# Pairwise sums of squares before the sums on TensorE, a later wait for the inverse root in two FFN blocks, and rows spread by two rounded products

## The reference, cut to what matters

```python
def rmsnorm(x, g):
    xf = x.astype(F32)
    y = xf * lax.rsqrt(jnp.mean(xf * xf, axis=-1, keepdims=True) + RMS_EPS)
    return (y * g.astype(F32)).astype(x.dtype)

def swiglu(h, w_in, w_out):
    a, b = jnp.split(h @ w_in, 2, axis=-1)
    return (jax.nn.silu(a) * b) @ w_out
...
        x = x + g1 * rmsnorm(y_lat, norm_g[l, 1])
        f_lat = swiglu(rmsnorm(x, norm_g[l, 2]) * (1.0 + sc2) + sh2, ffn_w_in[l], ffn_w_out[l])
...
    # gated_delta_rule, layer 3: g and beta are one row of 256 tokens for each of the 8 heads
    gc = jnp.cumsum(g, axis=-1)
    diff = gc[..., :, None] - gc[..., None, :]
    decay = jnp.where(tril, jnp.exp(jnp.where(tril, diff, 0.0)), 0.0)
    kb = k * beta[..., None]
    lmat = jnp.where(strict, jnp.einsum('nbhid,nbhjd->nbhij', kb, k) * decay, 0.0)
```

## Time and profile before

| | us |
|---|---|
| median of 3 runs | 2207.27 |
| lowest and highest | 2203.91, 2208.76 |
| the profiled execution | 2202.34 |
| its span in the trace | 2200.5 |
| TensorE busy | 2129.5 (97%) |
| VectorE busy | 1416.4 (64%) |
| ScalarE busy | 996.8 (45%) |
| GpSimd busy | 178.0 (8%) |

### The profile page before, as it was taken

The page is one execution under the profiler, slowest core; times in us unless marked ns, Lnnn a source line. Parts: engine busy times, 40 slices in busy tenths (PEclk is TensorE's granted clock), DMA queues, the critical chain, the costliest instruction groups (busy, mean ns, idle before and its releaser), DMA issues.

```text
span 2200.5 us, 32199 instructions
## 1 busy us (share of the span) xinstructions
PE 2129.5 (97%) x13450; PEld 1831.8 (83%) x13450; DVE 1416.4 (64%) x1612; ACT 996.8 (45%) x1124; POOL 178.0 (8%) x94
## 2 busy tenths in 40 slices
PE   6999998999999999999999999999999999989999
PEld 4887787888888856888888898888988897878888
DVE  4267974766756456666666678666666688566665
ACT  3322353544544244444544555445544566254444
POOL 0065600000000000000100011000100012001000
PEclk8999999999999999999999999999999999999999
DMA  8227924455455412455555534555455543124552
GB/s 337 97 96 301 421 88 146 170 189 190 163 190 188 157 72 77 155 189 191 196 189 190 189 134 144 191 191 191 156 190 190 190 154 116 41 87 172 191 191 77
DMA packets 52609, 373.28 MB, mean 170 GB/s; under 512 B 5792, under 2 KB 6816, under 8 KB 7968
## 3 DMA queue, kind: packets, MB, share of 16 engines
q1 hardware_dynamic: 51632, 367.71, 45.8%
q0 software_dynamic: 880, 4.19, 0.6%
HBM read 370.84 MB, written 1.05 MB: 169 GB/s over the span
## 4 chain that ended last, share of the span: by engine, by line
PE 45%; DVE 3%; ACT 2%; POOL 0%; issue 0%; ACTq 0%; DVEq 0%
PE PS L376 13%; PE PS L380 7%; PE PS L395 4%; PE PS L396 4%; PE PS L397 4%; PE PS L299 3%; PE PS L1498 1%; PE PS L286 1%; PE PS L288 1%; PE PS L287 1%; PE PS L2184 1%; DVE ring_r L500 1%; PE PS L1667 0%; PE PS L1769 0%; POOL X L1464 0%; PE PS L1457 0%
## 5 line engine op out<-in xcount | busy, mean ns | idle before, releaser
L500 DVE TENSOR_TENSOR ring_r<-ring,AR_r 128x2048 fp32r<-128x2048 f32 x290 | 664.5, 2298 | 263.8 <-ACT AR_r L494 263.6
L494 ACT ACTIVATE AR_r<-ring 128x2048 fp32r<-128x2048 f32 x290 | 552.6, 1911 | 327.2 <-PE PS L397 196.0
L376 PE MATMUL PS<-AR_r 128*128 128x512 f32 x2240 | 533.2, 390 | 0.0
L376 PEld LDWEIGHTS PS<-AR_r 128*128 128x128 f32 x2240 | 415.6, 188 | 83.1
L380 PEld LDWEIGHTS PS<-AR_r,ring_r 128*128 128x128 f32 x2240 | 287.2, 191 | 10.9
L380 PE MATMUL PS<-AR_r,ring_r 128*128 128x256 f32 x2240 | 290.6, 283 | 0.0
L541 ACT ACTIVATE AR<-PS 128x512 f32<-128x512 f32 x140 | 83.7, 598 | 420.5 <-PE PS L380 420.5
L396 PE MATMUL PS<-ring_r,AR_r 128*128 128x512 f32 x616 | 241.2, 392 | 0.0
L395 PE MATMUL PS<-AR_r 128*128 128x512 f32 x616 | 241.2, 392 | 0.0
L397 PE MATMUL PS<-AR_r 128*128 128x512 f32 x616 | 240.3, 390 | 0.0
L603 DVE TENSOR_TENSOR AR<-AR,PS 128x512 f32<-128x512 f32 x70 | 48.1, 687 | 141.3 <-ACT AR L541 141.3
(11 more groups left out here) (412 smaller groups left out, 2941.3 us busy)
## 6 DMA issues: line engine op xcount, KB each, us to landing
ring<-stream SPq DMA_DIRECT2D x346, 1024.0 KB, 4.8
X<-xt SPq DMA_DIRECT2D x1, 2048.0 KB, 9.7
AR<-bias POOLq DMA_DIRECT2D x1, 1536.0 KB, 7.0
AR<-pt POOLq DMA_DIRECT2D x2, 512.0 KB, 4.7
out<-X SPq DMA_DIRECT2D x4, 256.0 KB, 2.1
AR<-invc SPq DMA_DIRECT2D x1, 512.0 KB, 15.3
X<-negl POOLq DMA_DIRECT2D x1, 512.0 KB, 7.4
H<-wax POOLq DMA_DIRECT2D x1, 512.0 KB, 7.7
```

Of the source, the lines that this page charges most:

```text
L376: pe.matmul(PS[:, (6, 4)[half] + j, :], block(w_hi_of(tag, i + half), j, k), X_PARTS[:, k, :], start=(k == 0), stop=False, skip_group_chec ...
L494: act.activation(w_hi_of(tag, i), ring[:, n % SLOTS, :], ACT.Identity).then_inc(split_hi, 1)
L500: dve.tensor_tensor(RING_R[:, n % SLOTS, :], ring[:, n % SLOTS, :], w_hi_of(tag, i), ALU.subtract).then_inc(split_lo, 1)
```

## The change

1. **Pairs.** For the five later sums VectorE first adds the squares of the two feature tiles of a pair (new function `dve_pair_squares`, four TENSOR_TENSOR of 128x256, after `dve_add_turned`), and `pe_norm` makes four products in place of eight. The two sums that open the kernel stay.
2. **A sum one chunk earlier.** ("ffn0_pre", 0) now stands between the context chunks 1 and 2 of mixer 0's output projection, not between 2 and 3.
3. **A later wait in the two FFN blocks.** `sums` no longer waits for `rinv`. Banks 1 to 3 are opened at once, `down(0, 4, ...)` begins with them, and only ahead of bank 0 come the wait for `rinv` and the opening of bank 0.
4. **Rounded spreads.** ScalarE rounds ROWS to ROWS_HI once (8x512), VectorE makes ROWS_LO (8x512) and a rounded copy of the identity's corner (8x8), during the projections of mixer 3; `spread(h)` is two fp32r products of 512 columns in place of one in full fp32.

```diff
+            else:
+                for q in range(GROUPS):
+                    pe.wait_ge(S["paired_squares"], S.at("paired_squares", (tag, q)))
+                    ins = pe.matmul(PS[:, bank, 0:T], ONES, SQ[:, 2 * q, cols], start=(q == 0), stop=(q == GROUPS - 1))
             ins.then_inc(S["feature_sums"], S.mark("feature_sums", tag))
+        def dve_pair_squares(dve, tag, cols):
+            for q in range(GROUPS):
+                dve.wait_ge(S["squares"], S.at("squares", (tag, q)))
+                dve.tensor_tensor(SQ[:, 2 * q, cols], SQ[:, 2 * q, cols], SQ[:, 2 * q + 1, cols], ALU.add).then_inc(
+                    S["paired_squares"], S.mark("paired_squares", (tag, q)))
...
+                for t, h in ((0, 1), (1, 0), (1, 1), (0, 0)) if open_first else ((0, 0), (0, 1), (1, 0), (1, 1)):
+                    if open_first and (t, h) == (0, 0):
+                        open_first()
...
-                sums()
-                open_sums()
+                summed = sums()
+                for b in range(1, 4):
+                    pe.matmul(PS[:, b, 0:2], ZERO[:, :], ZERO[:, 0:2], start=True, stop=False, skip_group_check=True)
+                def open_first():
+                    pe.wait_ge(S["rinv"], S.at("rinv", summed))
+                    pe.matmul(PS[:, 0, 0:2], ZERO[:, :], ZERO[:, 0:2], start=True, stop=False, skip_group_check=True)
                 pe.wait_ge(ffn_gated, g0 + 1)
-                down(0, 4, False, 0)
+                down(0, 4, False, 0, open_first)
...
             out_chunk(1, ctx)
+            pe_norm(pe, ("ffn0_pre", 0), LAT, 0)
             out_chunk(2, ctx)
-            pe_norm(pe, ("ffn0_pre", 0), LAT, 0)
             out_chunk(3, ctx)
...
-                pe.matmul(PS[:, SPREAD_BANKS[h % 4], :], bc(IDENT[0:DH, h:h + 1], [DH, P]), ROWS[0:DH, :, :], start=True, stop=True).then_inc(S["row_spread"], S.mark("row_spread", h))
+                pe.wait_ge(S["cols_taken"], S.at("cols_taken", "rows split"))
+                row = bc(ONE_OF[0:DH, h:h + 1], [DH, P])
+                pe.matmul(PS[:, SPREAD_BANKS[h % 4], :], row, ROWS_HI[0:DH, :, :], start=True, stop=False)
+                pe.matmul(PS[:, SPREAD_BANKS[h % 4], :], row, ROWS_LO[0:DH, :, :], start=False, stop=True).then_inc(S["row_spread"], S.mark("row_spread", h))
...
+                    act.wait_ge(S["beta3"], S.at("beta3"))
+                    act.activation(ROWS_HI[0:DH], ROWS[0:DH], ACT.Identity).then_inc(S["rows3"], S.mark("rows3", "rounded"))
...
+                    dve.wait_ge(S["rows3"], S.at("rows3", "rounded"))
+                    dve.tensor_tensor(ROWS_LO[0:DH], ROWS[0:DH], ROWS_HI[0:DH], ALU.subtract).then_inc(order.sem, order.step())
+                    dve.tensor_copy(ONE_OF[0:DH], IDENT[0:DH, 0:DH]).then_inc(S["cols_taken"], S.mark("cols_taken", "rows split"))
...
             dve_add_turned(dve, order, "mix1_post", HIGH, LAYER1 + G_MIXOUT, 0)
+            dve_pair_squares(dve, "ffn1_pre", LAT)
             dve_modulate(dve, order, "ffn1_pre", 0, LAYER1 + G_FFN, LAYER1 + SH_FFN, "ffn1_lat")
```

More of the change, by code:

```diff
@@ L227, in pe_norm @@
             bank = norm_bank(cols) if bank is None else bank
-            for k in range(DT):
-                if k % 2 == 0:
-                    pe.wait_ge(S["squares"], S.at("squares", (tag, k // 2)))
-                ins = pe.matmul(PS[:, bank, 0:T], ONES, SQ[:, k, cols], start=(k == 0), stop=(k == DT - 1))
-            ins.then_inc(S["feature_sums"], S.mark("feature_sums", tag))
+            if tag[0] == "mix0":
+                for k in range(DT):
+                    if k % 2 == 0:
+                        pe.wait_ge(S["squares"], S.at("squares", (tag, k // 2)))
+                    ins = pe.matmul(PS[:, bank, 0:T], ONES, SQ[:, k, cols], start=(k == 0), stop=(k == DT - 1))
+            else:
+                for q in range(GROUPS):
+                    pe.wait_ge(S["paired_squares"], S.at("paired_squares", (tag, q)))
+                    ins = pe.matmul(PS[:, bank, 0:T], ONES, SQ[:, 2 * q, cols], start=(q == 0), stop=(q == GROUPS - 1))
+            ins.then_inc(S["feature_sums"], S.mark("feature_sums", tag))
+        def dve_pair_squares(dve, tag, cols):
[3 more added lines that the diff above has]
+                    S["paired_squares"], S.mark("paired_squares", (tag, q)))
         ADA_GROUPS, ADA_FIRST = 24, 4
@@ L2033, in build @@
         COLS = arena(24064, 2, 3, DH)
+        ROWS_HI, ROWS_LO = arena(24192, 2, T, of=AR_R), arena(23040, 2, T, of=AR_R)
+        ONE_OF = arena(24704, DH, of=AR_R)
         NA = TMP[0:DH, 0:2]
@@ L2642, in sums @@
                 pe_norm(pe, tag, cols, 0)
-                pe.wait_ge(S["rinv"], S.at("rinv", tag))
+                return tag
             for t in range(1):
@@ L2812, in _ @@
             dve_add_turned(dve, order, ("mix0_post", 0), LOW, G_MIXOUT, 0)
+            dve_pair_squares(dve, ("ffn0_pre", 0), LAT)
             dve_modulate(dve, order, ("ffn0_pre", 0), 0, G_FFN, SH_FFN, "ffn0_lat")
@@ L2815, in _, with add_and_pair @@
             dve_split_chunk(dve, "ffn0_lat", 2)
-            dve_ffn(dve, "ffn0_lat", lambda: dve_add_turned(dve, order, ("mix0_post", 1), LOW, G_MIXOUT, 1),
+            def add_and_pair(tag, g, s, nxt):
+                dve_add_turned(dve, order, tag, LOW, g, s)
+                dve_pair_squares(dve, nxt, STREAM[s])
+            dve_ffn(dve, "ffn0_lat", lambda: add_and_pair(("mix0_post", 1), G_MIXOUT, 1, ("ffn0_pre", 1)),
                     lambda: dve_modulate(dve, order, ("ffn0_pre", 1), 1, G_FFN, SH_FFN))
@@ L2822, in _ @@
             dve_split_chunk(dve, "ffn0_ctx", 2)
-            dve_ffn(dve, "ffn0_ctx", lambda: dve_add_turned(dve, order, "ffn0_lat", LOW, G_FFNOUT, 0),
+            dve_ffn(dve, "ffn0_ctx", lambda: add_and_pair("ffn0_lat", G_FFNOUT, 0, ("mix1", 0)),
                     lambda: dve_modulate(dve, order, ("mix1", 0), 0, LAYER1 + G_MIX, LAYER1 + SH_MIX))
             dve_rms_tokens(dve, order, "ffn0_ctx", 1, LOW, TOK1[0], need_tokens(dve, "ffn0_ctx", "ffn0_ctx", FFN_LAST))
-            dve_add_turned(dve, order, "ffn0_ctx", LOW, G_FFNOUT, 1)
+            add_and_pair("ffn0_ctx", G_FFNOUT, 1, ("mix1", 1))
             dve_rest(dve, order)
```

24 lines of the change are left out of this document (11 added, 13 removed).

## The result

| | before, us | after, us |
|---|---|---|
| median | 2207.23 of 4 | 2190.91 of 4 |
| lowest and highest | 2203.91, 2208.76 | 2186.96, 2192.62 |
| the profiled execution | 2202.34 | 2192.62 |
| its span | 2200.5 | 2190.8 |
| TensorE busy | 2129.5 | 2124.6 |

The changed kernel takes 0.9925 of the time before, with an interval from 0.991 to 0.994: faster by 16.3 us in the medians, where 16.3 was forecast. A second series of the same kernel, label e12_after_again, gave 0.9939, from 0.9924 to 0.9954: 13.4 us by this ratio against its own runs of before, 14.9 between the medians. The two profiled executions differ by only 9.7 us: before's was 4.9 under its median, after's is the highest of its four. So the forecast has to be checked place by place, not by its sum alone.

What follows compares the result with a forecast made beforehand. TensorE was taken as the bound, busy 2129.5 of 2200.5 us, with waits on chains through other engines. Gains 8.7 + 2.0 + 3.6 + 1.7 - 1.2 + 1.5 = 16.3 us off 2207.3 gave 2191.0, range 2183 to 2200.

Steps and rivals of the forecast that it cites:

- A: Sum ("ffn0_pre", 0) among mixer 0's context chunks: 8.7 us gained, 7.1 by the chain and 1.6 by the clock.
- B: Sum in "ffn0_lat": 2.0 us gained, with a new TensorE wait of some 0.7 ahead of gate_up(5).
- C: Sum in "ffn0_ctx": 3.6 us gained, or 2.0 if the clock falls anyway.
- D: Sum in the second mixer, where TensorE has no wait on either side: 1.7 us gained.
- E: Sum ahead of "ffn1_lat": 1.2 us lost (0.4 to 2.1), by late pair additions and a lower clock.
- F: Rounded spreads of mixer 3: 1.5 us gained, from a loss of 1.2 to a gain of 4.7.
- They cost nothing: Mixer 3's projections: the new rounding and two VectorE instructions add no time; without cover 0.8 us.
- Rival 1: The chain ahead of "ffn0_lat" binds elsewhere, gaining 3 to 4 us and not 8.7: 2196 us; chance 0.15.
- Rival 2: The clock takes back gains in both FFN blocks, ahead of "ffn1_lat" and in mixer 3: 2197.8 us; chance 0.12.
- Rival 3: The clock gives back: no fall in mixer 3 or ahead of "ffn1_lat", 21.1 us gained, 2186.2 us; chance 0.12.
- The other two: Every sum waits for its pairs, 2207 us; or the clock stays low into the FFN, 2220 us; chance 0.02 each.

Runs made afterwards that it cites:

- e12_after_again: The changed kernel unchanged, run again in a second series beside the combined kernel; 2189.88 us, 0.9939 of the time before.
- e3: The kernel before with the rounded spreads of mixer 3 alone; 2207.27 us, 1.0004 of the time before.
- e4: The kernel before with the later wait for the inverse root alone, all sums with eight products; 2204.12 us, 0.999 of the time before.
- e1: The changed kernel with the sum ("ffn0_pre", 0) back between context chunks 2 and 3; 2196.96 us, 0.9953 of the time before.
- e5: The kernel before with the five pairwise sums alone; 2201.15 us, 0.9978 of the time before.
- e11: The changed kernel with full-precision spreads again and one and two unused products of constants ahead of mixer 3's heads 2 and 3; 2184.60 us in one execution.
- e7: The changed kernel with four and three unused products of constants ahead of heads 2 and 3 of mixer 3; 2186.95 us, 0.992 of the time before.
- e6: The changed kernel with seven unused products of constants in the wait ahead of the "ffn1_lat" sum; 2189.62 us, 0.9932 of the time before.

## Why the prediction was right or wrong

**A, right.** Chain by 7.1, then TensorE's own chunk 3 with a wait of about 1.0 (0.71 came), and 1.6 from the clock: -8.8 for -8.7. How near that is owes something to before's execution, 0.9 shorter at this place than e3's and e4's. e1 shows the order's share, and that the clock's part comes and goes with the wait.

**B, C and D, right,** B to 0.1, with the reason foreseen: the split of chunk 5 takes the place of the wait for RI (0.76 for 0.7). In C the 1.6 us of clock did go. But I read it as C's own; e3 and e5 show that it falls on either block. Alone, the later wait is worth 0.2 a block at full clock, less than I had.

**E, mis-sized: the term "E costs 1.2".** Its order part was right (the sum started 3.80 us behind VectorE's first addition to X, 3.72 predicted, and e11 gives +0.5). I took the middle between a fall and none, 0.4 and 2.1. The fall came in every execution of after's code here but e11's, and it weighed in two ways: ScalarE's reading of the sum came 1.24 us later relative to the additions, and the 32 products behind started 6.38 ahead of the next where it was 5.29, 1.1 more. The second I had not counted. And the 1.7 that my 2.1 had for a sum wholly at 1.2 GHz was too much: the clock fell inside it, and it took 2.75 us, 0.8 over my 1.95. That the two errors cancel, 2.2 for 2.1, is luck. By the rule of the Trainium skill quoted in the prediction (page "TensorE: Matmul & The Clock Gate", section "HAM oscillation — how this bites in real kernels") E would lose its full 2.1. It lost 2.2 in after and 0.5 in e11 with the same code here: the traces agree in most executions, not in all.

**F, mis-sized: the term "F: 1.5" and the words "They cost nothing".** I had 0.6 for chunk 14 with the clock's return where it was, and went up to 1.5 for a sooner return. But I had two rounded products at 0.9 us at the lower clock, and they took 1.15 (1854.14 to 1855.29), so chunk 14 started 0.85 sooner behind `head_products(3)` and not 1.1. The clock came back only 0.6 us sooner (1860.15 less 1852.16 in after, 1870.83 less 1862.20 before, by the spacing of chunk 14's products), and 0.7 was gained. And the projections' extra instructions cost 0.6: I had asked whether the next split is due in time, not who else stands behind VectorE, which was the convolution, ScalarE, a bank and the turn.

**The range.** The low ends of the places add up to 6.3 us and the high ends to 21.2, not to the 7 and 22 that I wrote; that moves the two times about the median, 2185 and 2200, later by about 1 us each, and nothing else.

**The sum.** My misses of 1.0 and 1.3 us make the places' sum 2.3 us less than forecast. That the first median is exactly 2191.0 owes something to luck; the two series' gains of 16.3 and 13.4 us have intervals that hold both 13.9 and 16.3.

**The rivals.** Rival 1 is out by A's wait. Rival 2 (the clock takes back) came true in E alone, and not in B and C. In F it didn't: F came out at -0.2, and the loss of 1.2 that rival 2 had there was not reached. Rival 3's state of F and E is what e7 and e6 bring about. The other two didn't occur.

## What to carry to other kernels

Ask of a sum what stands behind it: ahead of a long chain its place in the queue was worth four times the saved products (6.7 us against 1.7, 1.3 of the 6.7 being the clock). Work added to an engine that is back to back has a price even where its nearest consumer has slack; follow every consumer down to the bank that it frees. And before products are taken away ahead of a wait, look at the clock in the next stretch: in two places here filling the wait gained more (3.2 and 3.6 us) than the saved products did.
